# GpSimd makes each weight unit's low half in four instructions instead of one: a two-layer hybrid encoder on one Trainium2 core

## The reference

```python
def conv_ffn(h, buf, w_up, conv_w, conv_b, w_down):
    z = h @ w_up                                   # 1024 -> 2 * 2816
    zc, new_buf = causal_dwconv(z, buf, conv_w)    # three taps over positions
    gate, up = jnp.split(zc + conv_b, 2, axis=-1)
    return (jax.nn.silu(gate) * up) @ w_down, new_buf
```

## Time and profile before

| | |
|---|---|
| time, median of 3 runs | 1632.49 us (1630.94 to 1635.48) |
| profiled execution, first to last instruction (span) | 1624.3 us |
| TensorE busy | 1547.9 us, 95% of the span |
| VectorE busy | 1058.9 us, 65% |
| ScalarE busy | 458.6 us, 28% |
| GpSimd busy | 512.5 us, 32%, of which the low halves (L345): 195 instructions, 485.9 us |
| mean granted TensorE clock | 0.984 of full speed |

### The profile page before, as it was taken

One profiled execution on the slowest core, in us unless ns is written; L12 is line 12 of the kernel. 1 busy time (PEld: TensorE's weight loads), 2 busy tenths in 40 slices (PEclk: granted clock), 3 DMA queues, 4 the chain that ended last, 5 costly groups with the idle time before them and its releaser, 6 DMA issues.

```text
span 1624.3 us, 26037 instructions
## 1 busy us (share of the span) xinstructions
PE 1547.9 (95%) x10292; PEld 1522.0 (94%) x10292; DVE 1058.9 (65%) x1313; ACT 458.6 (28%) x717; POOL 512.5 (32%) x221
## 2 busy tenths in 40 slices
PE   6999999999999999999998999998999999999995
PEld 5999998899999999999998999998999999999994
DVE  6556665755956666666767553368966666667667
ACT  4345664443212121212115111115211111121123
POOL 4322220243323333233233333333333323332331
PEclk8999999999999999999999999999999999999997
DMA  5211116222222222221222222212122222222211
GB/s 205 70 61 53 53 53 229 102 66 66 69 70 70 78 65 66 76 76 54 77 78 71 80 68 78 74 59 78 54 77 78 65 77 65 77 64 65 78 37 65
DMA packets 34873, 123.76 MB, mean 76 GB/s; under 512 B 3920, under 2 KB 6864, under 8 KB 33648
## 3 DMA queue, kind: packets, MB, share of 16 engines
q1 hardware_dynamic: 31872, 108.37, 21.2%
q10 hardware_dynamic: 2928, 14.35, 2.3%
HBM read 114.48 MB, written 8.22 MB: 76 GB/s over the span
## 4 chain that ended last, share of the span: by engine, by line
PE 74%; DVE 17%; DVEq 4%; issue 2%; ACT 1%; DMA 0%; POOL 0%; SPq 0%; ACTq 0%
PE ps L401 58%; PE ps L417 8%; DVE hh L972 4%; DVE x L761 3%; DVE y L965 2%; DVE y L961 2%; PE ps L484 2%; PE ps L584 2%; DVEq L1017 1%; DVE sq L728 1%; DVE xl L712 1%; DVEq L1002 1%; PE ps L536 1%; PE ps L691 1%; DVE zp L984 1%
## 5 line engine op out<-in xcount | busy, mean ns | idle before, releaser
L345 POOL TENSOR_TENSOR wl<-raw,wh 128x1024 fp32r<-128x1024 f32 x195 | 485.9, 2498 | 1003.1 <-ACT wh L1173 1003.1
L401 PE MATMUL ps<-xh,wh 128*128 128x328 f32 (+5 forms) x2176 | 506.5, 314 | 15.6 <-DVE xl L712 15.3
L401 PE MATMUL ps<-xl,wh 128*128 128x328 f32 (+5 forms) x2176 | 503.1, 313 | 0.0
L401 PE MATMUL ps<-xh,wl 128*128 128x328 f32 (+5 forms) x2176 | 502.7, 313 | 0.0
L401 PEld LDWEIGHTS ps<-xh,wh 128*128 128x128 f32 x2176 | 389.3, 190 | 18.8 <-issue 9.5
L401 PEld LDWEIGHTS ps<-xl,wh 128*128 128x128 f32 x2176 | 390.2, 190 | 0.0
L401 PEld LDWEIGHTS ps<-xh,wl 128*128 128x128 f32 x2176 | 389.5, 190 | 0.0
L1173 ACT ACTIVATE wh<-raw 128x1024 fp32r<-128x1024 f32 x196 | 204.3, 1055 | 346.6 <-PE ps L401 323.3
L417 PE MATMUL ps<-gh,wh 128*128 128x322 f32 (+1 forms) x800 | 186.3, 314 | 30.3 <-DVE x L761 30.2
L965 DVE SCALAR_TENSOR_TENSOR y<-zp,par,y 128x660 f32<-128x660 f32 (+1 forms) x192 | 185.6, 967 | 26.9 <-issue 22.1
L761 DVE TENSOR_TENSOR x<-ps,x 128x644 f32<-128x644 f32 (+2 forms) x208 | 161.7, 821 | 53.8 <-PE ps L417 28.7
(11 more groups left out here) (154 smaller groups left out, 1153.4 us busy)
## 6 DMA issues: line engine op xcount, KB each, us to landing
raw<-w_units SPq DMA_DIRECT2D x196, 512.0 KB, 3.5
s<-states ACTq DMA_DIRECT2D x4, 1024.0 KB, 5.3
state_sample<-snew ACTq DMA_DIRECT2D x4, 1024.0 KB, 4.1
x<-x_t SPq DMA_DIRECT2D x8, 328.0 KB, 6.5
x<-x_t ACTq DMA_DIRECT2D x1, 2624.0 KB, 11.4
y_t<-x SPq DMA_DIRECT2D x6, 320.0 KB, 2.4
ffn_last<-zl ACTq DMA_DIRECT2D x2, 396.0 KB, 2.4
zc<-ffn_cache ACTq DMA_DIRECT2D x1, 704.0 KB, 4.2
```

The costliest lines, as they stand in the source:

```text
L345: pool.tensor_tensor(wl[:, j, :, :], raw[:, j, :, :], wh[:, j, :, :].bitcast(F32), ALU.subtract).then_inc(sem["lo_done"], 1)
L401: mm = pe.matmul(ps[:, p, c:c + z - a], w[:, ring, k, :], v[:, k, a:z], start=(k == 0 and w is wh and v is hi), stop=(k == KT - 1 and w is ...
```

## The change

The subtraction that makes a low half is written as four instructions over two of the eight contraction slices each. The four lie in one queue behind one wait, and the last one raises `lo_done`.

```diff
 MIX_G = 4
+LOW_PIECES = 4
...
         def low(j, done):
             pool.wait_ge(sem["hi_done"], done)
-            pool.tensor_tensor(wl[:, j, :, :], raw[:, j, :, :], wh[:, j, :, :].bitcast(F32),
-                               ALU.subtract).then_inc(sem["lo_done"], 1)
+            for q in range(LOW_PIECES):
+                ms = slice(q * KT // LOW_PIECES, (q + 1) * KT // LOW_PIECES)
+                part = pool.tensor_tensor(wl[:, j, ms, :], raw[:, j, ms, :], wh[:, j, ms, :].bitcast(F32),
+                                          ALU.subtract)
+            part.then_inc(sem["lo_done"], 1)
```

## The result

The changed kernel takes 1585.7 us (median of 4 runs, 1578.6 to 1589.3), the kernel before on the same chip 1631.7 us (4 runs, 1626.1 to 1635.5): a ratio of 0.973, 95% interval 0.970 to 0.976. The forecast was 1588. The profiled execution of the changed kernel took 1585.8 us with a span of 1584.0, that of the kernel before 1626.1 with a span of 1624.3. Profile against profile 40.3 us are saved, against a sum of 44.1 in the prediction.

The account below looks back on a forecast made before the run. TensorE hardly stops and waits mainly for VectorE, which GpSimd's low halves hold up. Terms 23.0 + 3.7 + 7.6 + 5 + 4.8 = 44.1 us give span 1580, median 1588 us; range 1578 to 1612.

Parts of the forecast that it names:

- Who gets the turn: Between queued GpSimd pieces and VectorE instructions: the two take strict turns, one instruction each, so VectorE waits for one piece.
- The rival in which GpSimd keeps its turn over its four pieces: Each low half holds VectorE 2.76 us instead of 2.40, so the kernel gets slower: 1649 us; chance 0.05.
- The price of a piece: GpSimd's piece of 256 columns: estimated 0.72 us alone, 0.68 for each next piece, 0.59 after a VectorE turn.
- some 0.15: VectorE instruction meeting a low half: waits for its end, then needs its own time less some 0.15 us.
- Steady groups: Sixteen FFN-group waits: 1.5 us each (1.05 at the scaling, 0.45 at `hh`), 23.0 in all; bounds 7 and 26.5.
- low halves end 0.4 us later ... so that is covered: Cost of later low halves: none, since SyncE's refill and TensorE's unit have a whole ring of four units.
- the half-size rival: Low half ahead of L961 comes no earlier, or `hh` and `gh` lose more; 0.45 us a group, 1605 us; chance 0.2.
- First down projections: First down projection of each layer, ending a VectorE backlog: half the stalls covers the wait, 3.7 us; bounds 1.8 and 3.7.
- Norms: Sum of squares of the two later norms: additions end 3.8 us earlier each, 7.6 together; bounds 4 and 9.8.
- Clock: TensorE's 1.2 GHz stretches after waits: losses of 6.4 us, of which 5 are taken as gained; bounds 1.3 and 6.4.
- Start: First low halves holding an addition and the last two L712: turns gain 4.8 us; bounds 2 and 6.5.
- The offset of 8.2 us between span and median: Median of runs 1632.5 lies 8.2 above the profiled span of 1624.3; left as it is, so span 1580 becomes 1588.

Follow-up runs that it names:

- the kernel with whole low halves at the other units: Against the kernel before: four pieces at three of every six FFN units, one instruction for the other three and everything ahead of the second loop; 1592.5 us, ratio 0.978.
- The run repeated: The changed kernel run once more with no edit; 1579.5 us, span 1577.7.
- the mixture: Against the changed kernel: four pieces kept for the three low halves at the start, eight pieces in both GpSimd loops; 1569.1 us, ratio 0.965.

## Why the prediction was right, and where it was not

Who gets the turn: right. GpSimd's queued pieces and VectorE's instructions of two SBUF inputs alternate one by one; in the third norm five additions start at intervals of 1.29 to 1.30 us (858.31 to 863.50), where 1.30 was counted. The rival in which GpSimd keeps its turn over its four pieces is refuted by each of these rows. On this point the Trainium skill, SBUF — State Buffer, section "Who interferes with whom", says that the first to issue holds the shared pair for its whole instruction; the rows agree for one instruction, and show that pieces already queued do not count as issued. The price of a piece, 0.72, was an estimate; it takes 0.73 to 0.74. The runs have 0.46 at 128 columns, 0.74 at 256, 1.29 at 512, 2.40 at 1024, which is a fixed part of some 0.18 us and 2.2 ns a column. The estimate in proportion from the GPSIMD Engine Reference of the Trainium skill (section "Elementwise — side-by-side cycle accounting"), 0.56, was too low. The "some 0.15" by which a held instruction ends sooner than its own time fits `hh` and `gl`; for the scaling it is 0.27 (0.35 of 0.62), and the count by hand used the 0.35.

1. *Steady groups, 23.0; measured 18.3.* This is the term that was mis-sized. Its two parts were right (1.05 and 0.45 counted, 1.12 and 0.36 measured alone), and the kernel with whole low halves at the other units gives 11.94 + 12.05 less 1.5 for the clock at 1497, 22.5. What failed is the step "low halves end 0.4 us later ... so that is covered". It looked at TensorE and SyncE, who wait for the low half, and not at VectorE's scaling at 692.46, for which the whole low half had ended just in time. 0.32 us a group in sixteen groups is 5.1 us, where 4.2 (22.5 less 18.3) are missing. The waits there stay at 0.3 to 0.75 us instead of the 0 to 0.4 forecast. The upper bound of 26.5 was too low as well, since it summed the brackets: eight pieces gain 30.5 in these groups (14.80 and 17.25 less 1.5). This also answers the half-size rival: the low half ahead of the scaling came earlier by 0.81 us against VectorE's normalisation (from 0.47 behind it to 0.34 ahead), and by 1.14 with the earlier unit whole, where 1.2 to 1.4 were counted; the rival needed none.
2. *First down projections, 3.7; measured 3.4.* Right.
3. *Norms, 7.6.* The additions gain 3.80 in the third norm, exactly as counted, and the two waits fell by 8.2 (9.8 to 1.5); the stage as a whole gains 9.1. It was essential that half of the twelve pieces fall outside of the sum: with two pieces a low half all six fall in, and of the additions' 3.80 only 0.5 are left (12.0 us against 12.5).
4. *Clock, 5; measured 7.1.* All four stretches at 1.2 GHz behind the waits went; the bound of 6.4 was a little low. The run repeated shows that the same clock comes and goes in the attention, by 7 us from one execution to the next, and no term stood for that.
5. *Start, 4.8; measured 6.0* (5.2 in the second profile). The last L716 ends at 20.39, where 20.4 was counted, so the 4.8 are there. The rest lies behind it, and no term stood for it: 0.7 up to TensorE's first sum (31.69 before, 26.21 now), with a stretch at 1.2 GHz of 3.4 us in place of the 10.2 from 19.14 to 29.38, and 0.5 at 41.70, where a wait of 0.3 for VectorE is gone. How much of the 0.7 is the clock's was not separated. The start gains 8.5 without the low halves.

That the time came out 2 us from the forecast owes something to errors that cancel: the sum was 4 us too large, and the span it was made against belongs to a run of 1626.1, 6 us below the median of those shown. The offset of 8.2 us between span and median was not overhead; span and time of one execution differ by 1.8.

## What to carry to other kernels

Where two engines lock each other out for whole instructions, cut the long instruction of the engine that has time, so that the other waits for a piece and not for the whole; but look in the trace for places where the whole instruction just ended in time, since the same work in pieces ends later there. The gain stops at the wait that the late engine causes, and a cut too fine makes the cut engine the late one: here eight pieces were the best of those tried (with four at the start), sixteen made GpSimd late at both layers' first down projection. And compare the same instruction in two traces stage by stage, with a repeat of one kernel beside it, before any stage's difference is put down to the change.

## What else the rows show of the hardware

VectorE's copy `gh` (L980), with one input and its output in SBUF, takes turns too: 0.88 us at 702.26 beside a piece, 0.50 alone. The prediction counted a turn for it, though no row of before showed one (0.49 to 0.50 us each time). The additions with an input in PSUM (L765) keep 0.82 us beside pieces of every size, as before.

The clock in the attention stage: 6.8 us at 1.2 GHz in the profile before, 17 us and none in two profiles of the changed kernel, none with eight pieces, 17 with two. It does not follow the number of pieces: the mixture, with the same eight pieces in this stage, has 10.2. TensorE was busy for 35.87 of 36.00 us in the window with a granted clock of 0.86 and for 35.74 in the one with 1.00. What sets it off stays open.
